# Attention projections as three fp32r products of high and low parts, y of a scan by features, and 8 KB weight runs in the experts

## The reference

```
# layer 0, both streams (h: 768 rows of 1024 features)
h   = modulate(rms_norm(x, norm1_g), shift, scale)
qkv = h @ w_qkv                       # 1024 x 3072
q, k, v = rms_norm(q, q_g), rms_norm(k, k_g), v
o   = neighbourhood attention of 16 heads of 64 (context tokens: plain attention)
x   = x + gate * (o @ w_o)            # 1024 x 1024
# layer 1: two scans over the tokens (forward, backward), 16 heads, state S of 64 x 64
sk = S @ kk;  S = S * w - sk kka' + v kt';  y = S @ r
readout: y - mean(y), scaled by rsqrt(var(y) + eps), gain, bias, bonus, gate, @ w_o
# each layer ends in an expert-choice block: router, 16 experts, each with w1, w3, w2 of 1024 x 1024
# shift, scale and gate of both layers: silu(c) @ ada_w + ada_b, 12 column blocks of 512 per layer
```

## Time and profile before

| | |
|---|---|
| median of 3 runs | 4359.24 us (4352.11 to 4361.37) |
| the profiled execution | 4362.38 us, its span 4360.7 us |
| PE busy | 3927.9 us, 90% of the span |
| DVE, ACT, POOL busy | 1622.7, 1130.8, 448.8 us |
| chain that ended last | PE 78%, DMA 10%, DVE 6%, ACT 3% |
| DMA | 739.05 MB; 359824 of 360079 packets under 8 KB |
| mean granted PE clock | 0.929 of full speed |

### The profile page before, as it was taken

The page is one execution under the profiler, slowest core; times in us unless marked ns, Lnnn a source line. Parts: engine busy times, 40 slices in busy tenths (PEclk is TensorE's granted clock), DMA queues, the critical chain, the costliest instruction groups (busy, mean ns, idle before and its releaser), DMA issues.

```text
span 4360.7 us, 58179 instructions
## 1 busy us (share of the span) xinstructions
PE 3927.9 (90%) x25227; PEld 2271.9 (52%) x25227; DVE 1622.7 (37%) x3000; ACT 1130.8 (26%) x2147; POOL 448.8 (10%) x494
## 2 busy tenths in 40 slices
PE   7999979999989975488999798888989999989998
PEld 4447553333335444477887432224556754456764
DVE  2206441212241257655544312224644322644322
ACT  2116321111131267333342210001142211133211
POOL 2211020000000122110011100000002200001200
PEclk9999989999999987667897899999999999989999
DMA  6331118898872159633341599994103222012321
GB/s 240 119 133 63 62 73 318 326 368 321 323 275 104 49 182 310 198 111 85 94 125 54 222 399 409 409 409 148 49 1 133 96 85 86 32 39 97 106 84 41
DMA packets 360079, 739.05 MB, mean 169 GB/s; under 512 B 67824, under 2 KB 144096, under 8 KB 359824
## 3 DMA queue, kind: packets, MB, share of 16 engines
q1 hardware_dynamic: 348416, 697.93, 44.2%
q0 software_dynamic: 11408, 37.41, 2.5%
HBM read 673.39 MB, written 61.89 MB: 169 GB/s over the span
## 4 chain that ended last, share of the span: by engine, by line
PE 78%; DMA 10%; DVE 6%; ACT 3%; issue 1%; SPq 1%; POOL 1%; POOLq 0%; DVEq 0%; ACTq 0%
PE ps L62 74%; DMA raw<-in_moe_w_dram 7%; PE ps L66 3%; DMA b<-in_ada_w_dram 2%; DVE mx L75 1%; SPq L120 1%; DVE o L75 1%; DMA a<-in_ada_w_dram 0%; ACT c L72 0%; DMA c<-in_w_in_dram 0%; DVE spr L75 0%; DMA sa<-Ad 0%; DVE b L75 0%; DVE sT L75 0%; ACT oT L72 0%
## 5 line engine op out<-in xcount | busy, mean ns | idle before, releaser
L62 PE MATMUL ps<-raw,xinT 128*64 128x512 f32 (+1 forms) x4096 | 596.4, 494 | 54.9 <-DMA raw<-in_moe_w_dram 46.2
L62 PE MATMUL ps<-c,hT 128*128 128x512 f32 (+2 forms) x1024 | 420.0, 565 | 6.5 <-ACT hT L72 4.3
L62 PEld LDWEIGHTS ps<-raw,xinT 128*64 128x64 f32 (+1 forms) x4096 | 194.7, 124 | 436.9 <-issue 287.7
L62 PE MATMUL ps<-wp,hp 128*128 128x512 f32 x1536 | 362.2, 397 | 9.3 <-DVE wp L75 9.3
L62 PE MATMUL ps<-a,nahT 128*128 128x512 f32 x768 | 338.1, 597 | 5.7 <-ACT nahT L72 5.2
L62 PEld LDWEIGHTS ps<-wp,hp 128*128 128x128 f32 x1536 | 292.2, 190 | 76.7 <-DVE wp L75 9.8
L62 PEld LDWEIGHTS ps<-c,hT 128*128 128x128 f32 x1024 | 192.2, 192 | 201.2 <-issue 195.7
L62 PE MATMUL ps<-raw,hidT 128*64 128x512 f32 x1024 | 239.9, 604 | 16.6 <-DMA raw<-in_moe_w_dram 16.3
L62 PEld LDWEIGHTS ps<-a,nahT 128*128 128x128 f32 x768 | 144.1, 191 | 178.6 <-issue 177.9
L62 PE MATMUL ps<-c,oT 128*128 128x512 f32 x512 | 222.8, 592 | 1.4 <-ACT oT L72 1.4
L62 PE MATMUL ps<-xr,b 128*128 128x512 f32 (+1 forms) x432 | 161.4, 534 | 9.1 <-ACT xr L72 4.5
(11 more groups left out here) (464 smaller groups left out, 5693.6 us busy)
## 6 DMA issues: line engine op xcount, KB each, us to landing
raw<-in_moe_w_dram SPq DMA_DIRECT2D x384, 1024.0 KB, 9.8
c<-in_w_in_dram SPq DMA_DIRECT2D x28, 2048.0 KB, 9.1
a<-in_ada_w_dram SPq DMA_DIRECT2D x16, 2048.0 KB, 12.9
b<-in_ada_w_dram SPq DMA_DIRECT2D x8, 2048.0 KB, 10.2
a<-in_na_w_qkv_dram SPq DMA_DIRECT2D x6, 2048.0 KB, 18.9
c<-in_w_branch_dram SPq DMA_DIRECT2D x16, 512.0 KB, 4.2
c<-in_w_out_dram SPq DMA_DIRECT2D x4, 2048.0 KB, 9.0
c<-in_w_ple_gate_dram SPq DMA_DIRECT2D x4, 2048.0 KB, 8.0
```

Of the source, the lines that this page charges most:

```text
L62: return self.e.matmul(out, lhsT, rhs, start=start, stop=stop, skip_group_check=True) if self.e is not None else self
```

## The change

Three edits, and some that follow from them.

**Attention's projections.** A matrix in fp32 is split into a high part (ACT copies it to fp32r) and a low part (DVE subtracts the high part, rounded to fp32r), and the product becomes high by high, high by low and low by high: 24 fp32r matmuls in place of 8 in fp32. The class `Parts` holds one weight block: raw in ring slot i, high part in slot j, low part written over the raw one. A block is cut in four pieces, and the pieces of block n+1 are made on ACT and DVE beside the units g = 2 to 5 of block n (`ahead`). The activations get their parts (naxh and nahTr; naohigh and naolow in na_out) in six pieces at the stage's start. Two slots for each block leave none for ada: its blocks now go through one slot (`rest`) in the tile that later holds v, three beside each n below 4. In na_norm the first ada blocks share three slots, and block 0 of w_qkv is fetched between ada blocks 1 and 2 and split before ada block 3. na_out goes through all groups for n = 0 and then for n = 1.

```
+    def act(self, e, m):
+        ks = slice(2 * m, 2 * m + 2)
+        e.wait_ge(*self.ring.loaded(self.i))
+        for f in self.ring.free(self.j):
+            e.wait_ge(*f)
+        e.activation(self.high[:, ks], self.raw[:, ks], ACT.Copy).then_inc(...)
+    def dve(self, e, m):
+        e.wait_ge(*self.P.act.at('high', m, *self.name))
+        e.tensor_tensor(self.low[:, ks], self.raw[:, ks], self.high[:, ks].bitcast(F32), SUB).then_inc(...)
+    def pe(self, e, out, high, low):
+        for k in range(8):
+            e.wait_ge(*self.P.dve.at('low', k // 2, *self.name))
+            e.matmul(out, high(k), self.high[:, k], k == 0, False)
+            e.matmul(out, high(k), self.low[:, k], False, False)
+            ins = e.matmul(out, low(k), self.high[:, k], False, k == 7)
...
# na_norm, in_order
         for m in range(4):
+            if m == 3:
+                split()
             block(m)
# na_norm, SP
             ring.fetch(e, i, I['ada_w'][l][:, n * 512:n * 512 + 512])
+            if m == 1:
+                W.ring.fetch(e, W.i, I['na_w_qkv'][0][:, 0:512])
# na_qkv
-        if g in (1, 3):
-            block(2 * n + g // 2)
-        if g in (2, 4):
-            turn(2 * n + g // 2 - 1)
+        if g % 2 == 0 and n < 4:
+            block(3 * n + g // 2)
+        if g % 2 and n < 4:
+            turn(3 * n + g // 2)
+    def ahead(n, g, split, *e):
+        if g >= 2 and n < 5:
+            split(W[n + 1], *e, g - 2)
...
# na_attend: the parts of w_o's first block
+            if 38 <= u < 42:
+                O.act(e, u - 38)
+            if 39 <= u < 43:
+                O.dve(e, u - 39)
```

```
-                    e.matmul(P.psum[:, banks[h % 2], sh(h // 2)], G[:, h, i * 128:i * 128 + 128], vh(h), h < 2, False)
+                    e.matmul(across(b, h), vh(h), G[:, h, 128:256], h < 2, False)
+                    ins = e.matmul(across(b, h), state(h), hd(fm[q % 3][:, 1], h), False, False)
...
-                    ins = e.matmul(P.psum[:, b, sh(h // 2)], G[:, h, 384:512], XU[:, 1, sh(h)], False, True)
+                    ins = e.matmul(across(b, h), XU[:, 1, sh(h)], G[:, h, 384:512], False, True)
```

```
+def braid(k, n=128):
+    return slice(256 * (k // 2) + k % 2, 256 * (k // 2) + k % 2 + 2 * n - 1, 2)
...
-        e.dma_start(self.raw[:, u % self.nr], self.src[u].rearrange("(k p) n -> p k n", p=128)).then_inc(...)
+        e.dma_start(self.raw[:, u % self.nr], self.src[u].rearrange("(p k) n -> p k n", p=128)).then_inc(...)
...
-        cut = lambda ch, k: x[:, ch, k * 128:(k + 1) * 128]
+        cut = lambda ch, k: x[:, ch, braid(k)]
...
-                        ins = e.matmul(P.psum[:, b, :], hl[:, pt, i, k * 128:(k + 1) * 128], sel_of(gi, i), ...)
+                        ins = e.matmul(P.psum[:, b, :], hl[:, pt, i, braid(k)], sel_of(gi, i), ...)
```

More of the change, by code:

```diff
@@ L448, in na_norm, with in_order @@
     s_x = [P.sig(f"nax{i}_in") for i in range(3)]
-    def in_order(chunk, block, turn):
+    def in_order(chunk, block, turn, split):
         for m in range(4):
+            if m == 3:
+                split()
             block(m)
@@ L461, in skip, with nothing_more @@
         pass
+    def nothing_more():
+        pass
     def pe(e):
@@ L469, in pe @@
         pe_turns(P, e, ('prow',), [prow[:]], (P.dve, 'pcol'))
+        b, free = P.banks.take(('pwide',), (P.dve, 'pcol'))
+        for f in free:
+            e.wait_ge(*f)
+        for j in range(2):
+            ins = e.turn(P.psum[:, b, 24 * j:24 * j + 24], pwide[:, braid(j)], P.ident)
+        ins.then_inc(*P.pe.inc('pwide'))
         def chunk(ch):
@@ L574, in na_qkv @@
     mod_rows(P, d)
[L575 to L578, removed]
+    xh = P.sb([128, 8, 768], F32R, name="naxh", ctx=d)
+    blocks = [by_products(P, rest) for _ in range(12)]
     s_g = [P.sig("naq_g"), P.sig("nak_g")]
@@ L641, in act @@
             beside(n, g, lambda m: act_ada(P, e, 4 + m), skip, lambda w: act_gate(P, e, 0, w))
+            ahead(n, g, Parts.act, e)
+        e.wait_ge(*P.pe.at('weights', id(rest), blocks[-1]))
         for n in range(4, 6):
@@ L702, in na_qkv, with na_attend @@
     d.close()
-def na_attend(P, I, ring, qT, kT, v, oT):
+def na_attend(P, I, ring, held, O, qT, kT, v, oT):
     NS = 3
@@ L888, in pool @@
         for j in range(2):
-            e.wait_ge(*P.pe.at('weights', id(ring), held + j))
+            for f in ring.free(held[j]):
+                e.wait_ge(*f)
             for t in (2, 7):
@@ L911, in na_out @@
     tmp = kT[:].rearrange("p a b -> p (a b)")[:, 2048:2560]
-    loads = [by_products(P, ring) for _ in range(2)]
+    toks = lambda g: slice(g * 128, g * 128 + 128)
     s_in, s_out = P.sig("nares_in"), [P.sig(f"na_out{i}") for i in range(3)]
@@ L966, in sp @@
     def sp(e):
-        for n, i in enumerate(loads):
-            ring.fetch(e, i, I['na_w_o'][0][:, n * 512:n * 512 + 512])
+        for n in range(2):
+            O[n].ring.fetch(e, O[n].i, I['na_w_o'][0][:, n * 512:n * 512 + 512])
     P.stage(pe, act, dve, pool, sp)
@@ L2365, in pe @@
     def pe(self, e, what, c):
+        if what == 'mean':
+            e.wait_ge(*self.P.dve.at('y', self.last(c)))
+            for half in range(2):
+                pe_turns(self.P, e, ('rw_y', c, half), [self.y[:, c, (4 * half + j) * 128:(4 * half + j + 1) * 128] for j in range(4)],
+                         (self.P.dve, 'ycentred', c))
         if what == 'turn':
@@ L2872, in pe @@
         fence(P, e, 'rw_scan')
+        R.pe(e, 'mean', 0)
         def product(c, n):
```

219 lines of the change are left out of this document (139 added, 80 removed).

## The result

The changed kernel takes 4285.16 us (median of 4 runs, 4283.95 to 4295.38) beside 4360.31 for the kernel before on the same chip: a ratio of 0.9833, with a 95% interval of 0.9809 to 0.9857, so 75 us or 1.7% less. The forecast was 58.7 us less.

A forecast was written before the change was run, and what follows sets the result against it. PE was taken to bound na_qkv and moe0, DMA moe1. Attention -36.1, y by features -10.7 and weight runs -11.9 gave -58.7 us on the profiled 4362.4, or 4303.7; with the median 3.1 lower, 4301 us, range 4260 to 4340.

The forecast's parts named there:

- the long runs: moe1: 8 KB packets in place of 4 KB raise DMA from 409 to 420 GB/s, -11.9 us.
- the braid: Weight loads on PE that take every second column: costed at 0, with a bound of +29 us.
- its term: Scan and readout: y by features, less the new turns, sums to -10.7 us.
- The products of attention: na_qkv and na_out: fp32r matmuls at 0.231 us each save 1.33 us a group, -47.7 and -15.9 us.
- The start: Before na_qkv's first product: block 0's load and its parts delay PE from 42.45 to 52.9 us, +10.4 us.
- The end of each weight block: na_qkv: PE waits 2.7 us for the last low part on DVE at four block boundaries, +10.8 us.
- The one-slot ring, attend, na_out: Attention: ada loads through one slot cost nothing, copies in na_attend +4 us, PE's first wait in na_out +2.3 us.
- y by features: Scan: shorter products save 1.3 us an item, -11.7 us over nine items bound by PE.
- the seven items that I counted at half: Scan: seven items where PE waits for DVE's small inverses, counted at half the saving, -4.6 us.
- the clock as a rival: Scan: new small waits pull PE's clock down over seven items, +49 us, 4350 us; chance 0.12.
- The turns: Scan and rw_readout: new turns of y cost +3.3 us for three chunks and +2.3 us for chunk 0.
- fp32r at 0.215 us: Attention: rival that fp32r matmuls pace faster than the 0.231 us taken, giving 4282 us; chance 0.1.

The follow-up runs named there:

- e3: The kernel before with only attention's projections changed, the scan and weight-run edits undone: 4319.3 us, ratio 0.9916.
- e1: The changed kernel with y of the scan back by tokens (128 columns of G as weights, 64 of v streamed): 4317.2 us, ratio 0.9909.
- e7: The kernel before with only y of the scan changed to by features: 4326.5 us, ratio 0.9941.
- e4: The changed kernel with w_qkv's block 0 split ahead of ada block 2 and each block's fourth piece split beside unit 4: 4268.5 us, ratio 0.9801.
- e5: The changed kernel with y's 8 products of v by G made twice per item (64 weight columns, 128 streamed): 4303.2 us, ratio 0.9882.
- e2: The changed kernel with 4 KB weight runs and plain feature order back: 4296.8 us, ratio 0.9859.
- e8: The changed kernel with all 11 DVE steps of the small inverses right behind the gram's copies: 4249.0 us, ratio 0.9744.
- e6: The changed kernel with four more products per item in step y, by tokens (128 weight columns, 64 streamed): 4306.9 us, ratio 0.9891.
- e9: The changed kernel with w_qkv's parts earlier, small inverses' steps behind the gram's copies, and their next input fetched one group ahead: 4210.0 us, ratio 0.9657.
- e10: The changed kernel with parts earlier, inverses' steps early and their input fetched ahead, but y of the scan by tokens: 4233.6 us, ratio 0.9725.

## Why the prediction was right, and where it was not

4285.2 lies in the range, on the fast side of 4301, and the direction was the likeliest case. Attention came out as forecast (38 us in e3, where I had 36.1), the long runs gave 9.5 us in moe1 for 11.9 and lost about 3 to the braid, and the scan brought two to three times its term: 32 us by e1, 24 by e7 (the 40.9 of the table are one pair of profiles, with a grain of 10). The scan alone missed its term by 13 us or more, na_qkv and moe0 fell short of theirs by 4 us each the other way, and the total by medians missed by 16 (75 against 58.7). That it didn't miss by more is luck.

- *The products of attention*: right. 0.233 us where I took 0.231. The stage gained 32.5 us where the sum had 36.9: the 0.002 us make 1.7 of it over 864 matmuls, and the products below full clock behind two of the waits about 1.2 us each; the rest isn't traced. The bound of 0.215 didn't show. The Trainium skill, TensorE: Matmul & The Clock Gate, "Wait — 56ns, not 53.3ns?", gives 215.7 ns for 512 columns back to back; with a new weight load for each matmul this trace has 233.
- *The start*: 12.2 us against 10.4. The step that was short is the end of hT's copies, 41.3 us in place of 39.3: PE had waited 7.5 us for DMA, and its ada block ran at the lower clock (3.64 us for 64 matmuls, where the next block took 1.96). e4 shows that 3.7 us of it were in the order.
- *The end of each weight block*: right in kind and number, four waits of PE for DVE. 8.6 us against 10.8; e4 gained 12.5 from them.
- *The one-slot ring, attend, na_out*: no wait for DMA in na_qkv. na_attend and na_out came 2 us better than forecast: na_attend 2.9 us longer up to na_out's first product, where I had 4 + 2.3, and na_out 14.7 us shorter, where I had 15.9.
- *y by features*: the products cost what I had worked out, an item 17.00 us against the forecast 17.05, with a wait of 0.54 us before level 2 against 0.6. **The step that failed is the seven items that I counted at half, -4.6 us.** I had seen that PE waits for DVE there, and took it that a shorter PE is then partly hidden. But DVE's steps start only when PE's step s is done, so PE from x to s and DVE from the state to the copies add up, and y stands in between, so that its time is not hidden. e5 bears this out: with y made longer PE is idle for 20 us of the seven items, as in e2, e4 and e7 (19 to 20). At full clock the shape is worth 1.35 us an item, 9.5 in all. The seven items went from 166.8 to 145.0 us (148 to 149 in e2, e4 and e7), so 9 to 12 us more came with the clock. By an estimate from the table, the time at half clock fell from 64 to 24 us (30), and half of the difference, up to 20 us (17), is what that can be worth; PE's idle time, 19 us in place of 10, took part of it back. I had the clock as a rival with the wrong sign, the danger that new small waits pull it down; that it could come back was not among the cases.
- *The turns*, +5.6, were mis-sized too: the two items with turns are 2 us longer together, and the stretch from the last gram to moe1 is 99 to 105 us with y by features against 109 to 117 with y by tokens, over all profiles.
- *Long runs*: 420 GB/s as forecast, so the line through 2 and 4 KB packets held at 8. The stage gave 9.8 us against 11.9 (9.5 over all profiles). By an estimate from the 3 cycles per packet of the Trainium skill, DMA: Bandwidth & Descriptors, "Why small descriptors are slow (HBM only)", this step would be 1.2%; the runs show 2.7%. *The braid* cost about 3 us where I had 0: the loads of hl took 194 ns against 188 by the median, those of hid 209 against 140. Before, then after:

```profile
L62 PEld LDWEIGHTS ps<-sel,hl x288: 186/188/334, 612.1 to 2523.0; 128*128 128x128 f32 x144
L66 PEld LDWEIGHTS ps<-ident,hid x128: 137/140/144, 700.9 to 2943.3; 128*128 128x128 f32 x128
```
```profile
L62 PEld LDWEIGHTS ps<-sel,hl x288: 193/194/336, 580.4 to 2451.2; 128*128 128x128 f32 x144
L66 PEld LDWEIGHTS ps<-ident,hid x128: 194/209/220, 669.6 to 2863.5; 128*128 128x128 f32 x128
```

The rival that came nearest by its time, fp32r at 0.215 us (4282), was wrong: the number was right by another cause. What stays open: how much of the scan's gain is the clock's and how much the shape's, stretch by stretch, since both move together, and why moe0's routing took about 1 us more (84.4 us before, 85.8 after), which e2 and e3 have too (85.2), so that attention's edit and not the braid brings it.

## What to carry to other kernels

Where two engines wait for each other in turn, every microsecond that one saves between being released and releasing counts in full; read this off the order of both, not off their busy shares. If PE waits there, look at its clock behind the wait: half a clock can hide as "PE is busy". Then ask what the other engine does between its release and its answer, and whether that could stand in its idle time: here one row of four numbers (e8) was worth half as much as the whole change.

## What the runs showed of the hardware

- The granted clock in this scan follows the waits. With PE's short waits for DVE between the items it was 0.69 to 0.72 (y by tokens) or 0.88 to 0.90 (y by features; 0.82 in e6); with two of them left it was 0.96 (e8), and without them 1.00 with either shape (e9, e10). The Trainium skill, TensorE: Matmul & The Clock Gate, "HAM oscillation — how this bites in real kernels", tells of a kernel whose clock falls at each wait for DMA and of a loop order that cures it; here the waits were for DVE, and the runs agree.
- Busy alone didn't bring the clock back. In the kernel before PE was busy for all of 2060 to 2080 us at 0.50, with y products among its work that load 128 columns of weights and stream 64. In the changed kernel the clock returned within 6 us of work in which the y products streamed 128 columns over 64. e6 against e5 points the same way: 0.82 against 0.88, and lower stretches of up to 24 us against 10, for about the same added time. The runs don't show what in the kind of work makes the difference.
- One core drew 420 GB/s with 8 KB packets, 409 with 4 KB and 389 with 2 KB.
- A weight load of every second 4-byte column took 6 ns more for hl (fp32r, 194 against 188) and 69 ns more for hid (fp32, 209 against 140) than a contiguous one.
